# Two thirds of layer 0's modulation product moved from the start of a two-layer kernel into its scans

## The reference

```python
mod_p = silu(c_ctx) @ w_ada[l] + b_ada[l]        # 1024 x 6144 weights a layer: 24 MB
mod_s = silu(c) @ w_ada[l] + b_ada[l]
sh1, sc1, g1, sh2, sc2, g2 = split(mod, 6)
h = rmsnorm(x) * (1 + sc1) + sh1
u = h @ w_in                                     # conv | Fourier | RWKV-7 | 3 gates
y_rwkv, s_fin = rwkv_branch(...)                 # two scans over time: forward, then backward
merged = sum(sigmoid(gate_b) * branch_b)
x = x + g1 * (merged @ w_o)
h = rmsnorm(x) * (1 + sc2) + sh2
x = x + g2 * ffn(h)                              # dense in layer 0, top 2 of 8 experts in layer 1
```

## Time and profile before

| | us |
|---|---|
| median of 3 runs | 2129.2 (2127.11 to 2133.69) |
| the profiled execution's own time | 2132.36 |
| its span | 2130.6 |
| PE busy | 1874.4 (88%) |
| DVE busy | 1117.8 (52%) |
| ACT busy | 870.5 (41%) |
| POOL busy | 477.4 (22%) |
| mean granted clock | 0.927 |

### The profile page before, as it was taken

One profiled execution on the slowest core, in us unless ns is written; L12 is line 12 of the kernel. 1 busy time (PEld: TensorE's weight loads), 2 busy tenths in 40 slices (PEclk: granted clock), 3 DMA queues, 4 the chain that ended last, 5 costly groups with the idle time before them and its releaser, 6 DMA issues.

```text
span 2130.6 us, 40469 instructions
## 1 busy us (share of the span) xinstructions
PE 1874.4 (88%) x16416; PEld 1650.4 (77%) x16416; DVE 1117.8 (52%) x1609; ACT 870.5 (41%) x1273; POOL 477.4 (22%) x362
## 2 busy tenths in 40 slices
PE   4699797989998999997979598999599999999997
PEld 3498685878787999997958497979587777778775
DVE  0146466663323111014667775332478787888776
ACT  2044323223234344334441323323266666676654
POOL 0055000014344666655600002525000000000000
PEclk7599787999999999998979799999699999999998
DMA  9923426103242444443300001333587777888770
GB/s 308 326 80 120 159 80 207 34 10 118 87 145 85 124 120 124 142 125 84 114 1 3 4 4 42 110 100 98 182 289 261 263 268 273 293 295 290 258 254 30
DMA packets 225012, 314.75 MB, mean 148 GB/s; under 512 B 15584, under 2 KB 169574, under 8 KB 224742
## 3 DMA queue, kind: packets, MB, share of 16 engines
q1 hardware_dynamic: 217856, 306.22, 43.8%
q10 hardware_dynamic: 7014, 6.44, 1.1%
HBM read 310.53 MB, written 2.10 MB: 147 GB/s over the span
## 4 chain that ended last, share of the span: by engine, by line
PE 78%; DVE 12%; DMA 5%; ACT 2%; issue 2%; ACTq 1%; SPq 0%; DVEq 0%; POOL 0%
PE bank L559 76%; DMA ring<-in_w_ada 4%; PE bank L556 2%; DVE cvT L1577 1%; DVE S L1646 1%; DVE hT L1444 1%; DVE rs L1439 1%; DVE U L1674 0%; DMA xin<-in_x_sample 0%; DVE St L1692 0%; DVE hT L1451 0%; DVE xT L1470 0%; DVE e_w_rest L178 0%; DVE St L1689 0%; DVE yT L1764 0%
## 5 line engine op out<-in xcount | busy, mean ns | idle before, releaser
L1956 POOL TENSOR_TENSOR weights_rest<-ring,weights_rounded 128x512 fp32r<-128x512 f32 x344 | 462.9, 1348 | 670.5 <-ACT weights_rounded L1146 669.7
L178 DVE TENSOR_TENSOR e_w_rest<-e_raw,e_w_rounded 128x1024 fp32r<-128x1024 f32 (+1 forms) x324 | 351.7, 1132 | 46.2 <-ACT e_w_rounded L1380 37.7
L1146 ACT ACTIVATE weights_rounded<-ring 128x512 fp32r<-128x512 f32 x344 | 215.8, 630 | 382.6 <-PE bank L559 373.7
L1380 ACT ACTIVATE e_w_rounded<-e_raw 128x1024 fp32r<-128x1024 f32 (+1 forms) x324 | 312.8, 990 | 92.6 <-PE bank L559 86.5
L559 PE MATMUL bank<-h_rounded,weights_rounded 128*128 128x384 f32 x688 | 233.7, 340 | 31.4 <-DVE h_rest L1485 31.4
L559 PE MATMUL bank<-h_rest,weights_rounded 128*128 128x384 f32 x688 | 232.6, 338 | 0.0
L559 PE MATMUL bank<-h_rounded,weights_rest 128*128 128x384 f32 x688 | 232.3, 338 | 0.0
L559 PE MATMUL bank<-e_w_rounded,hG_rounded 128*128 128x512 f32 (+1 forms) x432 | 164.1, 380 | 15.3 <-DVE hG_rest L1914 14.3
L559 PE MATMUL bank<-e_w_rounded,hG_rest 128*128 128x512 f32 (+1 forms) x432 | 161.5, 374 | 0.0
L559 PE MATMUL bank<-e_w_rest,hG_rounded 128*128 128x512 f32 (+1 forms) x432 | 160.5, 372 | 0.0
L559 PEld LDWEIGHTS bank<-h_rounded,weights_rounded 128*128 128x128 f32 x688 | 131.3, 191 | 34.0 <-issue 33.2
(11 more groups left out here) (280 smaller groups left out, 3529.8 us busy)
## 6 DMA issues: line engine op xcount, KB each, us to landing
ring<-in_w_ada SPq DMA_DIRECT2D x96, 512.0 KB, 6.4
e_raw<-in_moe_w_down SPq DMA_DIRECT2D x90, 512.0 KB, 5.0
ring<-in_w_in SPq DMA_DIRECT2D x88, 512.0 KB, 4.7
e_raw<-in_moe_w_gate SPq DMA_DIRECT2D x72, 512.0 KB, 6.0
e_raw<-in_moe_w_up SPq DMA_DIRECT2D x72, 512.0 KB, 6.9
e_raw<-in_moe_w_gate SPq DMA_DIRECT2D x36, 384.0 KB, 5.7
e_raw<-in_moe_w_up SPq DMA_DIRECT2D x36, 384.0 KB, 4.0
ring<-in_ffn_w_gate SPq DMA_DIRECT2D x22, 512.0 KB, 4.9
```

What stands on the lines that cost most here:

```text
L178: eng.tensor_tensor(wl, e_raw[n % E_RAW][:, 0:kn * w], wr.bitcast(F32), ALU.subtract).then_inc(s("e_rest"), 1)
L1146: a(w_parts[n % NSLOT][0], raw, ACT.Copy).then_inc(*E.up("rounded_ready", *key))
L1380: a(e_w[n % E_PARTS][0][:, 0:kn * w], e_raw[n % E_RAW][:, 0:kn * w], ACT.Copy).then_inc(s("e_rounded"), 1)
L1956: pool.tensor_tensor(wl, raw, wr.bitcast(F32), ALU.subtract).then_inc(*E.up("rest_ready", *key))
```

## The change

Four things change.

1. At the start only chunks 0 to 3 (8 halves) are multiplied, copied and turned. The other 16 halves of layer 0 go ahead of layer 1's 24 in the generator, and in the list of ring blocks, so 40 halves are spread over layer 0's preparation and scans.
2. There are more places for them: 2 before `kks`, 1 before `lowrank(0)`, 1 before `kkn`, 1 after `fno1`, 5 after `fno2`; in each scan 2 after the state's transposes, 1 at the start of levels 2, 3 and 4, and 7 in the steps; after `lowrank(1)` 3 and then 2 more. The 40th comes after scan 1. `meanwhile(3)` behind it finds the generator empty and does nothing.
3. Groups 1 and 2 of layer 0 are copied by ScalarE after `exps(1)`, turned by TensorE between the 25th and 26th half, and added by VectorE after `prep(1)`. They have SBUF areas of their own (`ada_at`). Because layer 1's chunks go into the same banks 4, 5 and 6, the first chunk of each of its groups waits for the copy of layer 0's group (`ada_copied`); the first half of its chunk 4 is the 25th half.
4. Identity products are now issued only where `meanwhile` is called with `warm=True`. In layer 1 a step has one group of four instead of two.

```diff
-        add_ada(0)
+        add_ada(0, range(4))
...
             if l + 1 < DEPTH:
-                add_ada(l + 1)
+                add_ada(l, range(4, 12))
+                add_ada(l + 1, range(12))
...
             def ada(l, i):
+                if l > 0 and i % 4 == 0:
+                    pe.wait_ge(*at("ada_copied", l - 1, i // 4))
...
-                    for i in range(12):
+                    for i in range(4):
                         for _ in ada(0, i):
                             pass
-                    ada_turn(0)
-                next_ada = (1 for i in range(12 if l + 1 < DEPTH else 0) for _ in ada(l + 1, i))
+                    ada_turn(0, (0,))
+                parts_left = [(0, i) for i in range(4, 12)] + [(1, i) for i in range(12)] if l == 0 else []
+                next_ada = (1 for l_, i in parts_left for _ in ada(l_, i))
+                def meanwhile(n, warm=False):
+                    for _ in range(n):
+                        if next(next_ada, None) is None and warm:
+                            for _ in range(FILL):
+                                mm(psum[7][:, 0:P], ident, ident, True, True)
...
+                meanwhile(2)
                 b = begin("kks", l)
...
+                meanwhile(1)
...
                 lowrank(0)
+                meanwhile(1)
...
                     last.then_inc(*E.fill("fno1", l, j))
+                meanwhile(1)
...
                     last.then_inc(*E.fill("fno2", l, m))
-                for _ in range(8):
-                    next(next_ada, None)
+                meanwhile(5)
...
                         lowrank(1)
-                        for _ in range(9):
-                            next(next_ada, None)
+                        meanwhile(3)
+                        if l == 0:
+                            ada_turn(0, (1, 2))
+                        meanwhile(2)
...
+                    meanwhile(2)
                     for lev in range(1, LEVELS + 1):
+                        if l == 0 and 1 < lev < LEVELS:
+                            meanwhile(1)
...
                         else:
-                            meanwhile()
+                            meanwhile(1, True)
...
                         into_state(0, lambda q, c, h: U[q, u_slot(c), h, :], False)
-                        meanwhile()
-                        meanwhile()
-                    if d == 1:
-                        for _ in next_ada:
-                            pass
+                        meanwhile(2 if l == 0 else 1, True)
...
+                for _ in next_ada:
+                    pass
+                meanwhile(3)
...
                         exps(1)
+                        if l == 0:
+                            ada_copies(0, (1, 2))
...
                         prep(1)
+                        if l == 0:
+                            modulation(0, (1, 2))
```

More of the change, by code:

```diff
@@ L262, in build @@
         Xs = [cut(f"Xs{i}", o + 512 * i, 512) for i in range(2)]
+        ada_at = {(l, g): cut(f"ada{l}_{g}", o + 512 * (g - 1) if (l, g) in ((0, 1), (0, 2)) else used["adas"][0] + 512 * g, 512)
+                  for l in range(DEPTH) for g in range(3)}
         rs = cut("rs", o, T); o += 1024
@@ L412, in halves, with add_ada @@
                 add(key + (half,), cols(w, c0, n, 4 * half), last)
-        def add_ada(l):
-            for i in range(12):
+        def add_ada(l, chunks):
+            for i in chunks:
                 for half in range(2):
@@ L642, in ada, with ada_turn @@
                     yield
-            def ada_turn(l):
-                for g in range(3):
+            def ada_turn(l, groups):
+                for g in groups:
                     b = begin("adaT", l, g)
@@ L649, in ada_turn @@
                     for i in range(4):
-                        last = transpose(b[:, i * P:(i + 1) * P], adas[:, (4 * g + i) * P:(4 * g + i + 1) * P])
+                        last = transpose(b[:, i * P:(i + 1) * P], ada_at[l, g][:, i * P:(i + 1) * P])
                     last.then_inc(*E.fill("adaT", l, g))
@@ L792, in _ @@
                                 last.then_inc(*E.fill(*job))
-                    def meanwhile():
-                        if next(next_ada, None) is None:
-                            for _ in range(FILL):
-                                mm(psum[7][:, 0:P], ident, ident, True, True)
                     def chunk(c):
@@ L927, in _ @@
                 if l + 1 < DEPTH:
-                    ada_turn(l + 1)
+                    ada_turn(l + 1, range(3))
                 for m in range(KD):
@@ L1109, in _, with ada_copies @@
                 vectors(l)
-            def ada_copies(l):
-                for g in range(3):
+            def ada_copies(l, groups):
+                for g in groups:
                     act.wait_ge(*at("block_used", "ada", l, 4 * g + 3, 1))
-                    a(adas[:, g * 512:(g + 1) * 512], psum[4 + g][:, :], ACT.Copy).then_inc(*E.up("ada_copied", l, g))
+                    a(ada_at[l, g], psum[4 + g][:, :], ACT.Copy).then_inc(*E.up("ada_copied", l, g))
             def squares(l, which):
@@ L1329, in _ @@
                             act.wait_ge(*drained("gup", l, i))
-                        ada_copies(l + 1)
+                        ada_copies(l + 1, range(3))
                     if b_ == 2 and m > 0:
@@ L1496, in rest_prod, with modulation @@
                 tt(xl, fprod[m % 3], xr.bitcast(F32), SUB).then_inc(*E.up("prod_rest", l, m))
-            def modulation(l):
+            def modulation(l, groups):
                 ba = v("b_ada", l, 0, 48)
-                for g in range(3):
+                for g in groups:
                     dve.wait_ge(*filled("adaT", l, g))
@@ L1508, in modulation @@
                 dve.wait_ge(*E.latest())
-                for which, name in ((0, "norm1"), (1, "norm2")):
-                    for s_ in range(2):
+                for which, g, name in ((0, 0, "norm1"), (1, 2, "norm2")):
+                    for s_ in range(2 if g in groups else 0):
                         stt(modAs[:, l, which, :, s_], mods[:, l, 24 * which + 8:24 * which + 16, s_], 1.0,
-                            v(name, l, 0, 8), A, M).then_inc(*E.up("modA_ready", l))
+                            v(name, l, 0, 8), A, M).then_inc(*E.up("modA_ready", l, which))
             for l in range(DEPTH):
                 if l == 0:
-                    modulation(0)
+                    modulation(0, (0,))
                 dve.wait_ge(*E.latest())
@@ L1783, in _ @@
                 if l + 1 < DEPTH:
-                    modulation(l + 1)
+                    modulation(l + 1, range(3))
                 residual(lambda m: ("o", l, m), l, 16, 1)
```

6 lines of the change are left out of this document (3 added, 3 removed).

## The result

The changed kernel took 2073.1 us, median of four runs (2064.7 to 2076.4), against 2129.2 (2127.1 to 2133.7) for the kernel before: a ratio of 0.973 with an interval of 0.970 to 0.976. The profiled execution is the one of 2064.7 us, its span is 2062.9, and before it was 2130.6.

The account below looks back on a forecast made before the run. TensorE's work was taken as the bound, with `w_ada`'s landing rate setting the pace at the start. Terms summed to -61.4 us from 2132.4, giving 2071.0 for the profiled execution and 2067.8 for the median; range 2055 to 2082.

Parts of the forecast that it names:

- to the first level product, scan 0 and 1: Wait before the levels in both scans: two halves fit in TensorE's wait of 2.38 us, no cost.
- rest of layer 0: After scan 1: one half hides in a wait of 4.35 us and the gates' projection doesn't wait, 0.
- The start: Up to the first projection: sixteen halves fewer, -48.2 us, or -45 if some load is late.
- Before scan 0: Preparation up to `tok`: ten halves instead of eight, higher clock, `ark_ready` sooner; `tok` at 233.5 instead of 250.0, -16.5 us.
- The levels: Layer 0's scans: TensorE has no gap, so 2 x 3 halves cost their full length, +6.0 us.
- small term for the first products at the higher clock: First two products of the levels, layer 0: faster at the higher clock, 1.25 us a scan, -2.5 in all.
- Between the scans: Before scan 1: five halves instead of nine, the third waiting for ScalarE's copy, low clock; -7.1 us, bounds -8.3 and -5.
- The steps: Scan 1, layer 0: seven halves replace identity products; transfer waits and low clock as in scan 0, +4.9 us, outputs included.
- Layer 1: Its scans: fewer identity products lengthen waits, the clock may fall; +2 us, bounds 0 and +8.
- The rule that was set against this term: Trainium skill: short idle spells between product groups swing the clock; it favours layer 1 at low clock, 2086 us, chance 0.07.
- The ring falls behind: Rival, layer 0's scans: half of 16 places wait for transfers and lose clock, 33 us, giving 2093 us; chance 0.08.

Follow-up runs that it names:

- e2_work_only: Changed kernel with the five halves before and in the levels of each layer 0 scan replaced by `condp` identity products, without transfers there: 2092.9 us.
- e1_bursts: Changed kernel with the 40 halves at the old places only, deferred but not spread: 2104.8 us, 0.990 of the kernel before.
- after_again: The changed kernel, unchanged, run once more on another chip: 2075.8 us, 0.976 of the kernel before.
- e5_by_block: Changed kernel with modulation taken and ring slots given back by 0.5 MB block, each half in the levels split over two places: 2072.6 us.
- e10_split: Changed kernel with ring blocks of 2 rows by 512 columns, taken and given back block by block, halves in the levels split over two places: 2072.1 us.
- e9_rows_2kb: Changed kernel with `w_ada` ring blocks cut as 2 rows of inputs by 512 columns instead of 4 by 256, otherwise the same: 2076.5 us.

## Why the prediction was right, and where not

The forecast of 2067.8 us lies 5 to 8 us below the measured medians. In the profiled execution the terms came out like this, in us, by the difference of the two timelines:

| stretch | forecast | measured |
|---|---|---|
| start, to the first projection | -48.2 | -46.6 |
| to `tok` of scan 0 | -16.5 | -13.7 |
| to the first level product, scan 0 and 1 | 0 | -0.2, +0.8 |
| levels of scan 0 (3.0 - 1.25) | +1.8 | +6.1 |
| steps and outputs of scan 0 | 0 | -6.6 |
| between the scans | -7.1 | -7.4 |
| levels of scan 1 | +1.8 | +7.1 |
| steps and outputs of scan 1 | +4.9 | -0.8 |
| rest of layer 0 | 0 | +0.9 |
| layer 1's scans | +2.0 | -4.1 |
| behind layer 1's scans | 0 | -3.4 |
| sum, before rounding | -61.4 | -67.7 |

- **The start** was the term that carried the sum, and it held. The 1.6 us that are missing, and more, lie in `norm_sum`, whose 16 products took 7.8 us instead of 5.3, at a granted clock of 0.70 from 46 to 56 us, where it was 0.98 from 95 to 105 us before.
- **Before scan 0** the clock came up for `lowrank(0)`, as forecast (5.4 us, 5 expected). At `fno2` the prediction misread its row: it took 4.58 us for 1.2 GHz and counted -2.3, but the clock was up already, and it takes 4.61 us now. Windows of the kernel before:

```profile
223.76:228.34 4.58, 4.58 (x28) 3.89 (x32) 0.00 (x0) 0.49 (x1) 0.00 (x0) 1.00 0.00 0
```

  So `ark_ready` came 4.6 us sooner behind the first projection, not 7. And `tok` had to wait for the last two halves. The transfer of the first of them was issued at 178.2, when the halves behind `fno2` (from 177.09) gave slots back; they were taken up at 184.90 and 187.91, and `tok` started at 189.8, where 185 had been forecast, or 187 with what the start lacked.
- **The levels are the step that failed:** "TensorE has no gap, so each of the halves costs its full length". That length was right, 3.1 us a scan for 3.0. What came with it was not priced at all: while the transfers run that each half sets off, TensorE's own instructions come late, 4.5 to 6 us of gaps a scan, and the busy time grows by another 1.0 to 1.3. I had read the window of 4.00 busy us out of 4 as "no room", and not the 4 GB/s at its end as "no traffic to compete with". The small term for the first products at the higher clock (-1.25) was not too large: in `e2_work_only` the levels without the added products are 2.4 and 2.2 us shorter than before, about 1.5 of it in busy time. In `e1_bursts` (29.7 and 30.1 us) they were shorter too, at the old clock of 0.94, so part of this differs from one execution to the next.
- **Between the scans** each step came true, the low clock and the wait for the copy included.
- **The steps** were mis-sized: 3.6 us had been charged for the transfers and the low clock behind them, and it comes only where the clock falls. With the transfers and a clock of 1.00 the steps took 27.5 to 29.6 us in either scan (31.8 where 4.8 us of gaps stood in them); in the executions in which the clock fell they took 30.9 to 33.6, at 0.82 to 0.92, as in the earlier trace rows. And part of the low clock of those rows had nothing to do with a half: it was 0.59 from 296.2 to 300.0, with a DMA share of 0.02.
- **Layer 1:** nothing that shows by experiment, for +2.0. The rule that was set against this term did not decide: the steps with one group kept a clock of 0.99, with waits for the state of 0.8 to 1.8 us. The -4.1 and -3.4 us of the profiled execution, with nothing changed behind the scans, were not traced to a step; the granted clock of this stretch also differs between executions of one kernel.

So the failed step, +9.7 us on the two levels, was made up for in the profiled execution by a clock that stayed up in the steps of both scans. That the number came out so near is in this part luck. In the profiled execution of `after_again` the clock did not stay up in scan 1, the levels were longer still (39.1 and 40.6 us), and the span was 2074.0: these three stretches are 8 of the 11 us between the two. The other executions have no profile, so that the same holds the medians above the forecast is likely and not shown. No rival happened. "The ring falls behind" came nearest in kind, the transfers do cost TensorE time in the scans, yet by another way: once in scan 0's steps, for 1.75 us, was a half waited for.

## What to carry over

Filling the waits of the busiest engine with work from elsewhere pays for what it takes off the start, if what is moved stands where that engine waits anyway; here the same deferral was worth 21 us with bursts and over 50 spread. A stretch that is dense in short instructions is a bad place to set off a transfer, even one that nobody waits for: look at what the stretch moved before, and put the loads under long instructions or under waits. The changed kernel shows the first: from 464 to 877 us 121 GB/s are moved beneath products of 128x384, and not one wait there is put down to "issue". And take a term's size from several executions where the granted clock in its row isn't 1.00.

## What was not expected of the hardware

**TensorE runs out of instructions under DMA traffic.** With 2 to 5 MB moved in 35 us beneath 64x64 products at 28 ns each, gaps of up to 3.9 us stand at distances of 126 products or, within two products, a multiple, and each ends 1.2 to 1.6 us after a packet of 16 KB of instructions has landed. Without traffic the same products have 0 to 0.9 us of them a scan.

**A gap can take the clock with it, or not.** In the changed kernel one of 2.41 us in the steps of scan 1 left the granted clock at 1.00. The same place in its second run, with 2.37 us, windows of 2 us, columns as above:

```profile
376.00:378.00 2.00, 1.07 (x38) 0.80 (x30) 1.87 (x5) 0.00 (x0) 0.00 (x0) 1.00 0.91 302
378.00:380.00 2.00, 0.56 (x20) 0.56 (x24) 1.93 (x5) 0.00 (x0) 0.00 (x0) 1.00 0.93 287
380.00:382.00 2.00, 2.00 (x30) 1.79 (x22) 1.89 (x4) 0.00 (x0) 0.00 (x0) 0.59 0.94 260
382.00:384.00 2.00, 2.00 (x21) 1.67 (x20) 0.00 (x0) 0.60 (x1) 0.00 (x0) 0.50 0.82 253
```

The clock falls to its lower level just after the products resume. These steps took 33.5 us instead of 29.6; not all of it is this gap's, since the clock was at 0.50 from 364 to 366 us too.

**Products into different groups of 32 rows of a bank seem to overlap.** 32 products over four groups took 1.08 us, 16 over two groups 1.07 (`e5_by_block`), 16 over four groups 0.64 (`e10_split`, at 206.45), all at a granted clock of 1.00.

**Pieces of 2 KB are fetched faster than pieces of 1 KB.** 1 MB landed every 2.7 us in place of 3.0, in `e9_rows_2kb`, and every 1.36 us for half of it in `e10_split`.
